# Two projections behind each of two norms multiplied chunk by chunk together, with the sums and roots around them reordered

## What is computed

```
x  = x + gate1 * rms_norm(mix_out)                 # mix_out = merged @ w_o
h2 = rms_norm(x, g_pre_ffn) * (1 + scale2) + shift2
gt, up = split(h2 @ w_ffn_in)                      # 1024 -> 2 * 2816
x  = x + gate2 * rms_norm((silu(gt) * up) @ w_ffn_out)
h  = rmsnorm(x, norm1_g) * (1 + sc1) + sh1         # the second layer starts
q, k, v, u = split(h @ w_in)
```

## Time and profile before

| | us |
|---|---|
| median of 3 runs | 1330.11 (1329.69 to 1331.35) |
| the profiled execution, its own time | 1329.58 |
| its span, first to last instruction | 1327.9 |
| chain that ended last: on PE, on DMA | 54%, 29% of the span |
| PE busy | 1150.1 |
| DVE busy | 843.0 |
| ACT busy | 459.9 |
| POOL busy | 416.0 |

### The profile page before, as it was taken

How to read it: one execution, slowest core, us unless ns; L and a number is a source line. 1 busy time by engine, 2 the same in 40 slices (tenths; PEclk the granted TensorE clock), 3 DMA queues, 4 the chain that set the end, 5 groups by cost and what they waited for, 6 DMA issues and landing times.

```text
span 1327.9 us, 14556 instructions
## 1 busy us (share of the span) xinstructions
PE 1150.1 (87%) x4566; PEld 747.0 (56%) x4566; DVE 843.0 (63%) x1927; ACT 459.9 (35%) x1090; POOL 416.0 (31%) x351
## 2 busy tenths in 40 slices
PE   3899988988999999797979999987787877877776
PEld 3788877856899998674546555532332323333222
DVE  6453328536588888643399685775848668486455
ACT  2114021105323334433343444343343434334334
POOL 0000000002245553320054554544343543544310
PEclk9889988997999999898989999989898997989999
DMA  9556554553377776251499999999999999999994
GB/s 383 208 191 239 205 222 191 191 220 135 133 303 316 288 283 268 108 222 42 148 387 420 421 421 422 421 421 421 422 421 421 422 422 422 421 422 420 422 421 179
DMA packets 57228, 413.06 MB, mean 311 GB/s; under 512 B 6480, under 2 KB 6480, under 8 KB 7120
## 3 DMA queue, kind: packets, MB, share of 16 engines
q0 software_dynamic: 42912, 311.97, 57.1%
q1 hardware_dynamic: 14112, 100.10, 19.3%
q10 hardware_dynamic: 144, 0.26, 0.1%
HBM read 411.26 MB, written 1.05 MB: 310 GB/s over the span
## 4 chain that ended last, share of the span: by engine, by line
PE 54%; DMA 29%; DVE 10%; ACT 4%; issue 3%; POOL 0%; SPq 0%; DVEq 0%; ACTq 0%; POOLq 0%
PE ps L445 13%; PE ps L947 12%; DMA areaB<-in_experts,idx 11%; DMA gate_area<-in_experts,idx 7%; PE ps L458 6%; PE ps L460 5%; PE ps L459 5%; DMA hT<-in_experts,idx 3%; DMA mod_ring<-in_experts,idx 3%; PE ps L694 2%; DMA areaB<-in_mod_w 2%; DMA areaA<-in_experts,idx 2%; PE ps L528 2%; PE ps L546 1%; DMA ring<-in_stream 1%
## 5 line engine op out<-in xcount | busy, mean ns | idle before, releaser
L445 PE MATMUL ps<-hT,ring 128*128 128x256 f32 x672 | 155.1, 393 | 1.5 <-DMA ring<-in_stream 1.5
L947 PE MATMUL ps<-areaB,mod_sum 128*128 128x512 f32 x268 | 133.8, 634 | 24.5 <-ACT mod_sum L1263 24.5
L1256 ACT ACTIVATE act<-now 128x1 f32<-128x1 f32 x256 | 51.0, 199 | 285.8 <-DVE now L1960 284.1
L445 PEld LDWEIGHTS ps<-hT,ring 128*128 128x128 f32 x672 | 132.2, 198 | 22.2 <-DMA ring<-in_stream 1.9
L458 PE MATMUL ps<-hT_h,w_lo 128*128 128x256 f32 x416 | 120.7, 290 | 3.7 <-POOL hT_l L1331 2.3
L947 PE MATMUL ps<-gate_area,mod_sum 128*128 128x512 f32 x204 | 101.4, 637 | 24.1 <-ACT mod_sum L1263 24.1
L460 PE MATMUL ps<-hT_h,w_hi 128*128 128x256 f32 x416 | 120.0, 288 | 0.0
L1472 DVE SCALAR_TENSOR_TENSOR mod_sum<-mod_ring,cols,mod_sum 128x256 f32<-128x256 f32 x294 | 119.2, 482 | 0.0
L459 PE MATMUL ps<-hT_l,w_hi 128*128 128x256 f32 x416 | 118.9, 286 | 0.0
L1324 POOL TENSOR_TENSOR w_lo<-ring,w_hi 128x512 fp32r<-128x512 f32 x41 | 100.7, 2473 | 56.4 <-ACT w_hi L1042 56.2
L947 PE MATMUL ps<-ring,mod_sum 128*128 128x512 f32 x188 | 95.2, 631 | 21.0 <-ACT mod_sum L1263 21.0
(11 more groups left out here) (351 smaller groups left out, 2092.2 us busy)
## 6 DMA issues: line engine op xcount, KB each, us to landing
ring<-in_stream SPq DMA_DIRECT2D x79, 1024.0 KB, 5.9
mod_ring<-in_mod_w POOLq DMA_DIRECT2D x40, 1024.0 KB, 6.8
gate_area<-in_mod_w SPq DMA_DIRECT2D x3, 1024.0 KB, 13.2
areaB<-in_mod_w SPq DMA_DIRECT2D x3, 1024.0 KB, 23.1
mod_ring<-in_mod_w SPq DMA_DIRECT2D x2, 1024.0 KB, 6.0
mod_ring<-in_stream SPq DMA_DIRECT2D x2, 1024.0 KB, 9.9
small<-in_small SPq DMA_DIRECT2D x1, 1352.0 KB, 28.6
areaB<-in_experts,idx POOLq DMA_INDIRECT x67, 33.7
```

The source lines that it names most:

```text
L445: last = mm(ps[:, bank, b * T:(b + 1) * T], w[:, at:at + P], rhs[:, k, :], start=(k == 0), stop=(k == KC - 1))
L947: last = mm(ps[:, B3 + 2 * t + b, :], spread_w[n // FEW % 2][:, n % FEW, :], row[ROW_OF[n]][:, D + 512 * b:D + 512 * b + 512], start=first ...
```

## The change

PE multiplies gu 0 and gu 1 together, and later qk2 0 and qk2 1. For each chunk of hT it runs the twelve matmuls of both units, then takes the next chunk; before, it ran the whole of one unit and then the other. Each bank now has two sums open at once: only the first matmul of a bank has the start flag. The tiles' transposes are separate calls; at border 1 those of tile 0 come ahead of the sums of modulation units 20 to 23. The sums of units 24 to 27 move from behind gu 3 to behind gu 2. ACT, DVE and POOL take the squares, roots and splits in another order.

```
@@ PE @@
-            transposes_by_tile(1)
+            tile_transposes(1, 0)
             mod_units(*range(20, 24))
+            tile_transposes(1, 1)
...
-            gate_up(0, 0)
-            gate_up(1, 1)
+            def first_two(kind, new):
+
+                both = (parts(kind, 0), parts(kind, 1))
+                for k in (0, 4, 1, 5, 2, 6, 3, 7):
+                    hT_chunk(new, k)
+                    for j, w in enumerate(both):
+                        for b in range(2):
+                            at = (b * KC + k) * P
+                            last = mm3(ps[:, j, b * T:(b + 1) * T], [v[:, at:at + P] for v in w],
+                                       [v[:, k, :] for v in hT_parts], k == 0 and b == 0, k == KC - 1,
+                                       skip_group_check=True)
+                        if k == KC - 1:
+                            last.then_inc(unit_done, 1)
+
+            first_two("gu", 1)
             pe.wait_ge(hid_ready, 1)
             gate_up(2, 0)
+            mod_units(*range(24, MOD_FRONT))
             pe.wait_ge(hid_ready, 2)
             down(parts("dn", 0), True, False)
             gate_up(3, 1)
-            mod_units(*range(24, MOD_FRONT))
...
-            for j in range(4):
+            first_two("qk2", 2)
+            for j in range(2, 4):
                 w = parts("qk2", j)
-                if j >= 2:
-                    pe.wait_ge(evac, 23 + j - 1)
+                pe.wait_ge(evac, 23 + j - 1)
@@ ACT @@
             x_squares(1, 0)
+            x_square_root(1, 0)
             act.wait_ge(unit_done, DONE("wo", 3))
             y_square(1, 1, 1)
-            x_square_root(1, 0)
...
             y_square_root(2, 0)
-            x_squares(2, 0)
             act.wait_ge(unit_done, DONE("dn", PAIRS - 1))
             for b in range(2):
                 y_square(2, 1, b)
+            y_square_root(2, 1)
+            x_squares(2, 0)
+            x_squares(2, 1)
             x_square_root(2, 0)
-            y_square_root(2, 1)
-            x_squares(2, 1)
@@ POOL @@
             split_lo(SPLIT0)
+            split_lo(SPLIT0 + 1)
             hT_split(1)
-            split_lo(SPLIT0 + 1)
@@ DVE, residual_and_norm(n) @@
                 add_y(n, 0)
-                x_statistics(n, 0)
-                if n == 2:
+                if n == 1:
+                    x_statistics(n, 0)
+                    normalise_tile(n, 0)
+                else:
                     gate_y(n, 1, 0)
                 y_statistics(n, 1)
                 gate_y(n, 1, 1)
-                normalise_tile(n, 0)
                 add_y(n, 1)
+                if n == 2:
+                    x_statistics(n, 0)
                 x_statistics(n, 1)
+                if n == 2:
+                    normalise_tile(n, 0)
                 normalise_tile(n, 1)
@@ DVE @@
             residual_and_norm(1)
+            split_lo(SPLIT0 + 1)
             hT_part(1)
-            split_lo(SPLIT0 + 1)
...
             residual_and_norm(2)
+            hT_part(2)
             spread(2, modT[:, 64:72])
-            hT_part(2)
```

## The result

| | before | after |
|---|---|---|
| median of 4 runs on one chip | 1329.9 us (1326.83 to 1331.35) | 1320.26 us (1316.69 to 1321.04) |
| profiled execution, its own time | 1329.58 | 1316.69 |
| its span | 1327.9 | 1315.0 |
| PE, DVE, ACT, POOL busy | 1150.1, 843.0, 459.9, 416.0 | 1136.1, 842.6, 461.2, 416.1 |

The ratio is 0.9919 (95% interval 0.9893 to 0.9946): 10.8 us less, between 7.2 and 14.2. The forecast was 7.6 us less, 1322.5; on 1330.11 the ratio gives 1319.3, just under the low end of the range, 1319.5 (the median of the changed kernel itself, 1320.26, is a little above it). The direction was right and the gain was forecast too small.

A forecast was written before the change was run, and what follows sets the result against it. PE held 54% of the chain that ended last, DMA 29% in the expert stage. Gains 0.2 + 0.5 + 5.6 + 1.3 = 7.6 us off 1329.58 give 1322.0, forecast 1322.5 for the median; range 1319.5 to 1326, 8 in 10.

The forecast's parts named there:

- tile 1's norm earlier: Border 1: two tile 0 instructions leave DVE's path between the reciprocals, so tile 1's norm and transposes come 0.85 us earlier.
- new wait for hid_l: Border 1: both gu units end nearly together, so PE waits 1.2 us for hidden(0) before gu 2.
- moved sums, up to gu 5: Loop's first pass: 0.5 us from covering dn 0's split, 5.6 us from losing the stall on POOL's w_lo.
- y done to first qk2 chunk: Border 2: ACT squares tile 1's y first, so PE's first chunk comes at 543.1 in place of 544.07.
- 96 qk2 matmuls, up to Q: Border 2: the joint pair takes 14.0 us, ending at 557.1; the third unit then waits 0.2 us for bank 0's copy.
- The stall didn't stay: Rival, loop's first pass: something else holds POOL or DVE, 5.6 us is lost from the sum; 1328.1 us, chance 7%.
- the gain wasn't taken up behind: Rival, expert stage: busy with DMA throughout, it absorbs the gain and the time stays at 1330 us; chance 4%.
- the clock stayed low for 9 us at neither border: Rival, both borders: the clock stays low for about 9 us, giving 1325.5 us; chance 14%.
- I take about 5.7 us, near their mean: 27 matmuls slow: Both borders: low clock lasts about 5.7 us after PE's start, 27 matmuls slow and 69 fast, 14.0 us per pair.
- the early clock: Bound, both borders: about 4.1 us low, 19 matmuls slow and 77 fast, 13.3 us per pair; 9.0 gained, 1321.1 us.
- POOL first: Rival, border 1: POOL's split of gu 1 starts ahead of DVE's, PE starts 0.7 us sooner; 1321.8 us, chance 8%.
- a gain of 1.4 less the wait: Border 1: the joint gu pair ends at 334.7, 1.4 us earlier; after the 1.2 us wait, 0.2 us is left.

The follow-up runs named there:

- the experiments on the sums: Only the sums of units 24 to 27 moved, in the kernel before: 0.9943, 1322.92 us; the changed kernel with them back behind gu 3: 0.9955, 1323.55 us.
- POOL's splits as before: The changed kernel with POOL's split of gu 1 behind its four chunks of hT_l at border 1, DVE's staying ahead: 0.9944, 1319.82 us.
- the tiles' order as before: The changed kernel with border 2's squares, roots and norms of the two tiles in the old order, transposes apart, qk2 0 and 1 together: 0.9946, 1321.8 us.
- an overlong filler: The changed kernel with matmuls nobody reads in PE's gaps at border 1, before the last modulation sums and at border 2: 0.9945, 1320.93 us.

## Why the prediction was right and wrong

Each step counted from W, forecast and measured in the first pair of profiles:

| step | forecast, us | measured, us |
|---|---|---|
| tile 1's norm earlier | 0.85 | 0.87 |
| first gu matmul later | 0.7 | 0.70 |
| the 96 gu matmuls | 14.0 | 13.78 |
| new wait for hid_l | 1.2 | 1.01 |
| gain up to gu 2 | 0.2 | 0.64 |
| moved sums, up to gu 5 | 6.1 (0.5 + 5.6) | 5.97 |
| last down | none | -1.6 |
| y done to first qk2 chunk | 0.96 | 0.97 |
| 96 qk2 matmuls, up to Q | 0.4 (0.6, of which 0.2 given back) | 2.81 |
| head, before W | none | 3.8 |
| behind Q | none | 0.4 |

In the kernel before, the 96 gu matmuls took 16.13 us; that, less the second, third and fourth row, is the gain up to gu 2, with the first row already inside the second. The forecast's 1.3 for border 2 is its 0.96 and its 0.4. From the gain up to gu 2 to the qk2 matmuls, the rows add up to the forecast's 7.6 (but for rounding) and to 8.8 measured.

**Right.** The mechanisms and nearly all sizes: the order of the norm, DVE first on the ports and POOL behind it, the start 0.7 later, the wait of one microsecond at gu 2, and the stall on POOL's split, which went whole and whose removal the experiments on the sums confirm from both sides. None of the rivals came. The stall didn't stay, the gain wasn't taken up behind, and the clock stayed low for 9 us at neither border.

**Wrong.** The step that failed is "**I take about 5.7 us, near their mean: 27 matmuls slow**", used at both borders alike. I took the time for which the clock stays low as a property of the pair of units. In these profiles it goes with what PE did ahead of the pair, and my own norm step changed that: with tile 0 held back, the 16 transposes stand in one row. At border 2 none was slow in 6 of 8 profiles with the row (27 and 19 in the others); with the transposes in two pieces 14 to 34 were, in all 7 profiles. In the 7 profiles with the row in which the pair began at the high clock, the granted clock had fallen 2.7 to 3.6 us ahead of the row and rose within 0.4 us of its end. In the one with 19 slow matmuls (POOL's splits as before) it fell only 1.0 us ahead of the row and rose 5.6 us behind its end. What put the fall there isn't shown. The forecast gave the pair 14.0 us and 0.2 for the copy of bank 0 behind it; together they took 11.76, 2.4 less. This is the term that was mis-sized. At border 1, 21 or 22 were slow, not 27; the rise came 4.6 us after PE's start, and 9 us in the kernel before, where PE stood for 0.5 us in the low stretch.

The Trainium skill (TensorE: Matmul & The Clock Gate, "Part 4: PE-mode transpose") says that a transpose doesn't count as busy time for the clock in the way of a matmul. By that the row of transposes should have changed nothing. These profiles speak against it for float32 transposes, though the run with 19 slow matmuls shows that the row alone doesn't decide it, and only one run, the tiles' order as before, varied it by itself.

**Also wrong:** the sum was made against one execution and the spread within the kernel was not asked for. Its border 2 was of the quick kind, 14 slow matmuls and none in the last down; the mean of five is 1.7 us slower from W to Q. The range took in the clock's time at the two borders, but not that a stretch of unchanged code may differ by 5 us between executions (W from 305.1 to 310.4). Its low end doesn't follow from its own sum: the early clock with 9.0 and POOL first with 0.7 make 9.7 us, or 1320.4, not 1319.5. Finally, that the joint order helps at border 1 was my reason for a gain of 1.4 less the wait. It is a loss of 1.1: what gained there was the norm's order and the lack of the hole. Not run is the pair apart with gu 1's splits behind the chunks as before; whether PE would then start earlier isn't shown.

## What to carry to other kernels

Look for waits in one engine's queue that stand behind a load or a sum it doesn't need: moving 16 tiny matmuls one unit ahead gave more than half of this gain. Where PE idles between dependent stages, count the matmuls of the next stage that run at double duration and see what stands directly ahead of them: drawing its small work together went with 2.1 us here, beside the 1.0 of the reordered steps themselves. Filling the gap with matmuls nobody reads brought 1.2 us at border 2 and 0.7 at border 1, and an overlong filler lost 4.9; size it from a row and let it end before the data comes. Multiplying two units chunk by chunk paid where PE would have outrun the chunks (border 2), and cost where the next unit waited for the first one's result (border 1).

## What the runs showed of the hardware

- A wait of 0.36 to 0.50 us in a stretch of matmuls went with a later rise of the granted clock or with its fall: 9 us against 4.6 at border 1, 27 slow matmuls against none at border 2. It need not: in two profiles of the kernel before, PE waited 0.55 us in the low stretch of border 2 and the clock was high right behind it, 4.1 us after the start. And without any wait 19 matmuls were slow there in one run.
- A float32 matmul of 128 x 512 shows as two records. At the high clock the next record begins 0.43 us later (ten in 4.45 us), at the low clock 0.86; a row of six that began at the low clock took 7.09 us. 16 transposes took 3.67 us at the low clock and 1.97 at the high one.
- The same code may take 305.1 or 310.4 us from the start to W on the same kernel, with the granted clock from 160 to 180 us at 0.83 in the slower one and 0.91 in the quicker; from 200 to 220 us it was 0.83 in both.
- The change repeats to 0.1 us from W to Q in its three profiles (239.68, 239.72, 239.79), while the times of all its executions go from 1314.86 to 1321.55. A stretch between two fixed points told apart what the medians couldn't.
